# Eight experts in the order of their counts, three of them with stationary blocks of 64 high and 64 low columns, weights in rows of 4 KB, and a quarter of the weight residuals on GpSimd

## The chip, the cores and the metric

The kernel runs on one core of a Trainium2 chip. The metric is the device time of one execution in microseconds; the time before is the median of three runs. A difference of 0.2% (about 4 us) is what a measurement of this kernel can tell from none.

## What is computed

Two transformer blocks in a row on 256 tokens of width 1024, in fp32, each of two layers. The last layer of the second block ends in a mixture of experts, and only that part concerns the change:

```python
def swiglu(h, w_gate, w_up, w_down):
    a = jnp.einsum('bsd,df->bsf', h, w_gate)
    u = jnp.einsum('bsd,df->bsf', h, w_up)
    return jnp.einsum('bsf,fd->bsd', jax.nn.silu(a) * u, w_down)

logits = jnp.einsum('bsd,de->bse', h.astype(F32), w_router.astype(F32))
top_val, top_idx = lax.top_k(logits, TOP_K_EXPERTS)          # 2 of 8
top_w = jax.nn.softmax(top_val, axis=-1)
combine = jnp.sum(jax.nn.one_hot(top_idx, N_EXPERTS, dtype=F32) * top_w[..., None], axis=-2)
for e in range(N_EXPERTS):
    out = out + combine[..., e:e + 1].astype(h.dtype) * swiglu(h, w_gate[e], w_up[e], w_down[e])
```

Gate and up are 1024 x 2816 for each expert, down is 2816 x 1024: 34.6 MB an expert, 277 MB in all. An expert sees only the tokens that the router gives it, 64 of 256 on average.

## The kernel before

The program is written out by hand, one instruction stream per engine, with semaphores between them. What stands ahead of the experts (the four layers' projections and attention, three MLPs and the router, 1142 us) is the same before and after.

**Products in parts.** TensorE works on fp32r values. Each fp32 factor is split into a high part (a copy rounded to fp32r, made by ScalarE) and a low part (the factor less its high part, a subtraction on VectorE). A product of two factors is three matmuls: high x high, high x low, low x high (`product`). In the experts, the stationary operand is a block of 128 listed tokens and the moving one the weights, 512 columns at a time.

**Weights.** A weight tile is 128 x 2048 fp32 (1 MB). SyncE loads it in two halves of 512 KB into one of six raw slots (`raw(s)`, in `slab`; `MORE_RAW`), ScalarE writes `w_hi` (L1892), VectorE `w_lo` (L977) into one of three split slots, and TensorE uses both (L2351 to L2353). SyncE may refill a raw slot when `lo_dve` says that the subtraction is done, ScalarE may refill a split slot when `w_used` says that TensorE is through with it. An expert has 33 tiles. Gate and up are cut in steps of 512 inner columns (the first one 256), so a row of such a tile in HBM is 2 KB (the first 1 KB); rows of down are 4 KB.

**One expert.** For each step j of the inner width: up and gate products into banks 1 and 0 (`rows_up`), SiLU on ScalarE (L2279), the product of both on VectorE (L1757), a turn by TensorE (transposes, L2470), high and low parts of the turned hidden rows (`hid_hi` on ScalarE, L2179; `hid_lo` on VectorE, L1559), and the down products of step j - 1, which fill the time between (`sums`, into banks 2 and 3). The order on each engine is written out in `body`, for VectorE so:

```python
step(0, ahead=int(first))
if last:
    last_lists(n)
else:
    lists(2 * i + p + 1, n + 1)
step(1, ahead=1)
if not last:
    make_index(1 - p, n + 1, not first)
```

**Tokens.** `lists` compares each token's place with 0 to 127, which gives TensorE a matrix to find the listed tokens' numbers (`list_places`); `make_index` writes them; GpSimd fetches the 128 rows of the next expert by an indirect DMA (`fetch`, L918), and adds an expert's 128 output rows to `y_rows` in HBM by another (`scatter`, L924). This is all that GpSimd does in the experts. ScalarE scales the output with the token's weight (`output`, L2263). The experts come in the order 0 to 7, in a loop over pairs (`each_expert`). The last one's output is added on chip, and the sums of the other seven are read back and folded into x (`by_gate`, `fold`, L1713 and L1718). If an expert has over 128 tokens, everything runs a second time for the rest (`flag`).

In the layers ahead, GpSimd does make low parts, of whole tiles in four instructions of a quarter each (L826), and VectorE and GpSimd share the lot by tile.

## Time and profile before

| | before |
|---|---|
| median of 3 runs | 1914.62 us (1911.88 to 1915.4) |
| profiled execution, first to last instruction | 1912.1 us |
| experts in it | 1142.6 to about 1892.5 us, 750 us |
| one expert in its middle | 93.7 us |
| busy: TensorE, VectorE, ScalarE, GpSimd | 1824.1, 1416.6, 1122.6, 392.8 us |
| DMA | 506 MB, 265 GB/s on the mean, 380 in the experts |

The profiled execution's own time is given by its span alone, 2.5 us less than the median. The page says for each engine what it was busy, and follows the chain of waits that ended last; the groups give for each line of the kernel its busy time, the mean of one instruction and the idle time just ahead of it with what ended it. A wait costs something only on the engine that sets the end.

### The profile page before, as it was taken

How to read it: one execution, taken by the hardware profiler on the slowest of the kernel's cores; microseconds unless marked ns; L12 is line 12 of the kernel's file. 1: busy time of each engine (PE TensorE's matmuls, PEld its weight loads, DVE VectorE, ACT ScalarE, POOL GpSimd, SP SyncE). 2: the span in 40 equal slices, each digit the busy share in tenths (PEclk: the TensorE clock that was granted, in tenths of full speed). 3: DMA queues.
4: the chain of work that ended last, by engine and by line, in shares of the span. 5: the costliest groups of instructions: out<-in, count | busy, mean ns of one | idle time of the engine just before them, and what ended most of it. 6: DMA issues, size and time to landing. Idle time of an engine off the chain costs nothing.

```text
span 1912.1 us, 26024 instructions
## 1 busy us (share of the span) xinstructions
PE 1824.1 (95%) x8799; PEld 1486.2 (78%) x8799; DVE 1416.6 (74%) x1631; ACT 1122.6 (59%) x1296; POOL 392.8 (21%) x315
## 2 busy tenths in 40 slices
PE   7899999989999998899989879999999999999997
PEld 6678886868888786688878667888888888888885
DVE  5748874466976586644458758889888888888897
ACT  6745444564443464443345537777777777777775
POOL 3722203463212363200046500000000000000000
PEclk9999999999999999999999989999999999999999
DMA  8348884418987341455544258999999999999994
GB/s 271 111 161 327 343 342 147 149 54 323 344 347 275 91 152 45 154 195 179 192 154 142 69 187 334 386 376 386 380 384 376 383 383 381 380 374 381 381 387 167
DMA packets 237934, 506.45 MB, mean 265 GB/s; under 512 B 23304, under 2 KB 74720, under 8 KB 231712
## 3 DMA queue, kind: packets, MB, share of 16 engines
q1 hardware_dynamic: 225664, 492.91, 70.9%
q0 software_dynamic: 3008, 10.32, 2.0%
q10 hardware_dynamic: 9184, 2.23, 0.5%
q8 instruction: 43, 0.70, 0.1%
q14 instruction: 35, 0.29, 0.0%
HBM read 497.49 MB, written 7.91 MB: 264 GB/s over the span
## 4 chain that ended last, share of the span: by engine, by line
PE 83%; DVE 7%; issue 6%; ACT 3%; POOL 1%; DMA 0%; POOLq 0%; SPq 0%; DVEq 0%; ACTq 0%
PE bank L2351 25%; PE bank L2353 25%; PE bank L2352 25%; PE bank L2470 2%; ACT slab L2042 1%; PE bank L2789 1%; DVE slab L1290 1%; PE bank L2561 1%; PE bank L2539 1%; ACT w_hi L1892 1%; PE bank L2521 1%; POOL w_lo L826 1%; DVE x L1074 0%; PE bank L2572 0%; DVE slab L1271 0%
## 5 line engine op out<-in xcount | busy, mean ns | idle before, releaser
L977 DVE TENSOR_TENSOR w_lo<-slab,w_hi 128x2048 fp32r<-128x2048 f32 x369 | 847.8, 2308 | 214.3 <-ACT w_hi L1892 213.3
L1892 ACT ACTIVATE w_hi<-slab 128x2048 fp32r<-128x2048 f32 (+2 forms) x421 | 796.6, 1898 | 329.0 <-PE bank L2353 256.3
L2351 PE MATMUL bank<-w_hi,hT_hi 128*128 128x512 f32 (+3 forms) x1664 | 649.4, 390 | 14.2 <-DVE hT_lo L1012 4.4
L2352 PE MATMUL bank<-w_lo,hT_hi 128*128 128x512 f32 (+3 forms) x1664 | 638.0, 383 | 0.0
L2353 PE MATMUL bank<-w_hi,hT_lo 128*128 128x512 f32 (+3 forms) x1664 | 637.9, 383 | 0.0
L2351 PEld LDWEIGHTS bank<-w_hi,hT_hi 128*128 128x128 f32 x1664 | 316.0, 190 | 77.9 <-DVE w_lo L977 8.8
L2353 PEld LDWEIGHTS bank<-w_hi,hT_lo 128*128 128x128 f32 x1664 | 315.5, 190 | 59.7
L2352 PEld LDWEIGHTS bank<-w_lo,hT_hi 128*128 128x128 f32 x1664 | 316.3, 190 | 55.3
L826 POOL TENSOR_TENSOR w_lo<-slab,w_hi 128x512 fp32r<-128x512 f32 (+2 forms) x208 | 262.4, 1295 | 381.3 <-ACT w_hi L1892 361.6
L2351 PE MATMUL bank<-w_hi,hid_hi 128*128 128x512 f32 x680 | 265.6, 391 | 0.7 <-DVE w_lo L977 0.7
L2353 PE MATMUL bank<-w_hi,hid_lo 128*128 128x512 f32 x680 | 265.0, 390 | 0.0
L2352 PE MATMUL bank<-w_lo,hid_hi 128*128 128x512 f32 x680 | 264.5, 389 | 0.0
L2351 PEld LDWEIGHTS bank<-w_hi,hid_hi 128*128 128x128 f32 x680 | 127.6, 188 | 29.2 <-issue 2.3
L2353 PEld LDWEIGHTS bank<-w_hi,hid_lo 128*128 128x128 f32 x680 | 127.6, 188 | 26.7
L2352 PEld LDWEIGHTS bank<-w_lo,hid_hi 128*128 128x128 f32 x680 | 127.7, 188 | 26.3
L924 POOL DMA_INDIRECT y_rows<-slab,posi x7 | 16.6, 2367 | 515.6 <-ACT slab L2263 515.6
L901 POOL TENSOR_TENSOR slab<-slab 128x512 f32<-128x512 f32 x32 | 60.0, 1893 | 251.6 <-ACT slab L2188 251.6
L1577 DVE SCALAR_TENSOR_TENSOR big<-slab,csilu,big 128x2048 f32<-128x2048 f32 x42 | 103.5, 2473 | 0.0
L2042 ACT ACTIVATE slab<-slab,att 128x256 f32<-128x256 f32 x144 | 71.4, 499 | 52.3 <-DVE att L1271 43.0
L2179 ACT ACTIVATE hid_hi<-bank 128x512 fp32r<-128x512 f32 (+1 forms) x95 | 47.6, 527 | 46.1 <-PE bank L2470 46.1
L1290 DVE TENSOR_TENSOR slab<-slab,att 128x512 f32<-128x512 f32 x56 | 52.7, 942 | 5.8
L1271 DVE CUSTOM_DVE_ANT_0 slab<-bank,const 128x256 f32<-128x256 f32 x88 | 31.9, 417 | 33.4 <-PE bank L2521 33.3
(252 smaller groups left out, 1232.0 us busy)
## 6 DMA issues: line engine op xcount, KB each, us to landing
slab<-in_w_exp_gate SPq DMA_DIRECT2D x176, 512.0 KB, 7.0
slab<-in_w_exp_up SPq DMA_DIRECT2D x176, 512.0 KB, 7.5
slab<-in_w_exp_down SPq DMA_DIRECT2D x176, 512.0 KB, 7.1
slab<-in_w_ada SPq DMA_DIRECT2D x48, 1024.0 KB, 5.5
slab<-in_w_mlp_in SPq DMA_DIRECT2D x64, 512.0 KB, 5.4
slab<-in_w_mlp_out SPq DMA_DIRECT2D x64, 512.0 KB, 9.0
slab<-in_w_in SPq DMA_DIRECT2D x56, 512.0 KB, 5.0
slab<-in_w_out SPq DMA_DIRECT2D x32, 512.0 KB, 4.6
```

Source lines behind the costliest of these rows:

```text
L826: ins = pool.tensor_tensor(w_lo[:, q, o], raw(s)[:, o], w_hi[:, q, o].bitcast(F32), ALU.subtract)
L901: pool.tensor_tensor(scr(X_ACT2 + t * F_UP, F_UP), a, a, ALU.mult).then_inc(sq_done, 1)
L977: dve.tensor_tensor(w_lo[:, q, 0:n], raw(s)[:, 0:n], w_hi[:, q, 0:n].bitcast(F32), ALU.subtract).then_inc(lo_dve, 1)
L1290: dve.tensor_tensor(p, p, r[:, s, :].unsqueeze(2).broadcast_to([P, TT, SEQ]), ALU.mult).then_inc(nrm_done, 2)
L1577: ins = dve.scalar_tensor_tensor(acc, w, c, acc, ALU.mult, ALU.add)
L1892: act.activation(w_hi[:, q, 0:n], raw(s)[:, 0:n], ACT.Copy).then_inc(hi_done, 1)
L2042: act.activation(p, p, ACT.Exp, bias=att[:, 1, j, t:t + 1], scale=-1.0, accum_out=att[:, 2, j, t:t + 1]).then_inc(ex_done, 1)
L2179: act.activation(to_hi[:, f0:f0 + n, t * P:(t + 1) * P], src, ACT.Copy).then_inc(hidh_done, 1)
L2351: pe.matmul(dst, a_hi, b_hi, start=start, stop=False)
L2352: pe.matmul(dst, a_hi, b_lo, start=False, stop=False)
L2353: return pe.matmul(dst, a_lo, b_hi, start=False, stop=stop_)
L2470: ins = pe.transpose(dst[t][:, f * P:(f + 1) * P], scr(src + t * width_ + f * P, P), ident)
```

## The change

It reorders and recuts the experts. What stands ahead of them changes in nothing but the width of the first two expert tiles.

- **Order.** Expert 0 stays first. The other seven are sorted by their number of tokens: the four with most take places 1, 3, 5 and 7, the three with fewest 2, 4 and 6. The sort (`sort`, 25 small instructions) runs on VectorE in the first expert; SyncE reads the expert's number for each place from `order`.
- **Short experts.** Places 2, 4 and 6 hold at most 64 tokens. The 128 stationary columns are their 64 high and 64 low columns side by side, so that two matmuls (with `w_hi` and `w_lo`) give the whole product, with its high rows in partitions 0 to 63 and its low rows in 64 to 127. ScalarE moves the latter down, VectorE adds them, for gate and up. The down products of the third block of inner columns are done in the next body with three matmuls, with `hid_lo` set to zero. The output's two halves are added to `y_rows` by two indirect DMAs, the second after the first has landed.
- **Tiles.** The inner width is cut in three blocks of 768, 1024 and 1024 columns. A tile of gate or up holds two k rows of the whole block, so its rows in HBM are 3 or 4 KB. An expert has 36 tiles: eight of 1536 columns (the ones numbered -4 to 3 in a body), 26 of 2048, two of 1024 (18 and 19, a down chunk loaded in two halves of 64 partitions). The matmuls of the first block are 384 columns wide.
- **Low parts.** For the 27 tiles in `QUARTERED`, VectorE subtracts the first three quarters and GpSimd the last one; TensorE and SyncE wait for both.
- SiLU and the other steps on a block come in two halves, and the first expert of each round uses banks 6 and 7 for its second up block.

```diff
+E_WIDTH = (768, 1024, 1024)
+E_FROM = (0, 768, 1792)
+MS = len(E_WIDTH)
+MT = 36
+SHORT = P // 2
+SHORT_AT = (2, 4, 6)
+QUARTERED = tuple(range(0, 9)) + tuple(range(14, 18)) + (20,) + tuple(range(23, MT))
+ROUND_SUMS = 16 * (3 + 4 + 2 * 3)
...
+def down_chunks(j):
+    return ((0, 2), (2, 2), (4, 1), (5, 1)) if j == 0 else ((0, 2), (2, 2), (4, 2), (6, 2))
...
+def tile_width(r, first, last):
+    if r in (18, 19):
+        return D
+    return 2 * E_WIDTH[0] if r < 4 or first and r < 8 or r >= MT - 4 and not last else TILE
...
+                def wide_rows(w, j, n, r0):
+                    for b in range(4):
+                        to, loaded = slot_free(n, r0 + b)
+                        d = to[:, 0:2 * E_WIDTH[j]].rearrange("p (k n) -> p k n", k=2)
+                        for k in range(2):
+                            sp.dma_start(d[:, k:k + 1, :], w[:, 2 * b + k:2 * b + k + 1, E_FROM[j]:E_FROM[j] + E_WIDTH[j]]
+                                         ).then_inc(loaded, 16)
+                def down_rows(w, j, n):
+                    for b, (f, nf) in enumerate(down_chunks(j)):
+                        to, loaded = slot_free(n, down_tile(j) + b)
+                        d = to.rearrange("p (i n) -> p i n", i=2)
+                        at = E_FROM[j] // P + f
+                        for i in range(2):
+                            if nf == 2:
+                                sp.dma_start(d[:, i:i + 1, :], w[:, at + i:at + i + 1, :]).then_inc(loaded, 16)
+                            else:
+                                o = slice(i * P // 2, (i + 1) * P // 2)
+                                sp.dma_start(d[o, 0:1, :], w[o, at:at + 1, :]).then_inc(loaded, 16)
...
+                    if n == n0 + 1:
+                        sp.wait_ge(order_done, 1)
+                    wg, wu, wd = weights(0 if first else sp.value_load(order[0:1, n - n0:n - n0 + 1], min_val=0, max_val=NE - 1))
...
+    def scatter(n, n0):
+        turn_, at = n0 // NE, n - n0
+        pool.wait_ge(yo_done, 2 * (n - turn_) + 2)
+        done = sums_after(turn_, at // 2, at % 2)
+        for a, o in enumerate((slice(0, SHORT), slice(SHORT, P)) if at in SHORT_AT else (slice(0, P),)):
+            pool.wait_ge(scattered, done - (16 if at not in SHORT_AT else 32) + 16 * a)
+            pool.indirect_dma_start(y_rows, bass.IndirectOffsetOnAxis(index[n % 2][0:o.stop - o.start, 0:1], 0), y_out[o, :], None,
+                                    compute_op=ALU.add).then_inc(scattered, 16)
...
+    def last_quarter(n, r, first, last):
+        pool.wait_ge(hi_done, EXPERT0 + MT * n + r + 1)
+        w = tile_width(r, first, last)
+        o, s, q = slice(3 * w // 4, w), raw_slot(r), split_slot(r)
+        pool.tensor_tensor(w_lo[:, q, o], raw(s)[:, o], w_hi[:, q, o].bitcast(F32), ALU.subtract).then_inc(lo_pool, 1)
     def expert_rows(n0):
         for n in range(n0, n0 + NE):
-            p = n % 2
-            if n > n0:
-                scatter(1 - p, n - 1, n0)
-            if n < n0 + NE - 1:
-                fetch(1 - p, n + 1, n0)
-        sums_back(n0 // NE)
+            first, last = n == n0, n == n0 + NE - 1
+            def quarters(r0, r1):
+                for r in range(r0, r1):
+                    if quartered(r):
+                        last_quarter(n, r, first, last)
+            quarters(0 if first else -4, 10)
+            if not first:
+                scatter(n - 1, n0)
+            if last:
+                sums_back(n0 // NE)
+            quarters(10, 22)
+            if n == 0:
+                pool.wait_ge(rows_out, 32)
+            if not last:
+                fetch(n + 1, n0)
+            quarters(22, MT if last else MT - 4)
...
+            mark(dve.tensor_copy(rank_at[:, 0:1], iota[:, 0:1]))
+            mark(dve.tensor_copy(rank_at[:, 1:NE:2], iota[:, 1:1 + NE // 2]))
+            mark(dve.tensor_copy(rank_at[:, 2:NE:2], iota[:, 1 + NE // 2:NE]))
+            mark(dve.memset(spare, 0.0))
+            mark(dve.tensor_copy(counts[:, 1:NE], tot[:, 0, 1:NE]))
+            link(dve.memset(counts[:, 0:1], 2.0 * SEQ))
+            link(dve.memset(spare[:, 2:NE:2], float(P - SHORT)))
+            mark(dve.tensor_tensor(at, across(counts), down_(counts), ALU.is_gt))
+            link(dve.tensor_tensor(same, across(counts), down_(counts), ALU.is_equal))
+            link(dve.tensor_tensor(same, same, k_("earlier", NE, NE), ALU.mult))
+            link(dve.tensor_tensor(at, at, same, ALU.add))
+            link(dve.tensor_reduce(turns, at, AX.X, ALU.add))
+            link(dve.tensor_tensor(at, across(turns), down_(rank_at), ALU.is_equal))
+            each = at.unsqueeze(1).broadcast_to([P, TT, NE, NE])
+            for src, to in ((wts, ranked_wts), (pos, ranked_pos)):
+                link(dve.tensor_tensor(picked, each, src.unsqueeze(2).broadcast_to([P, TT, NE, NE]), ALU.mult))
+                link(dve.tensor_reduce(to, picked, AX.X, ALU.add))
+            link(dve.tensor_tensor(same, at, across(iota[:, 0:NE]), ALU.mult))
+            link(dve.tensor_reduce(turns, same, AX.X, ALU.add))
+            dve.tensor_copy(order[:, :], turns[0:1, :]).then_inc(order_done, 1)
...
+                def lows(r0, r1):
+                    for r in range(r0, r1):
+                        w, s, q = tile_width(r, first, last), raw_slot(r), split_slot(r)
+                        w = 3 * w // 4 if quartered(r) else w
+                        dve.wait_ge(hi_done, n * MT + (EXPERT0 + r + 1))
+                        dve.tensor_tensor(w_lo[:, q, 0:w], raw(s)[:, 0:w], w_hi[:, q, 0:w].bitcast(F32), ALU.subtract
+                                          ).then_inc(lo_dve, 1)
+                def activated(j):
+                    at = ub + n * (2 * MS) + 2 * j
+                    banks = (bank[6], bank[7]) if first and j == 1 else (bank[4], bank[5])
+                    w = half_of(j)
+                    if short:
+                        base = half_base(turn_, i, j)
+                        for c, o in enumerate(halves(j)):
+                            dve.wait_ge(half_moved, base + c + 1)
+                            dve.tensor_tensor(mact[0:SHORT, o], bank[c][0:SHORT, 0:w], mact[0:SHORT, o], ALU.add
+                                              ).then_inc(half_added, 1)
+                        for c, o in enumerate(halves(j)):
+                            dve.wait_ge(half_moved, base + c + 3)
+                            dve.tensor_tensor(up_low[:, o], banks[c][0:SHORT, 0:w], up_low[:, o], ALU.add
+                                              ).then_inc(half_added, 1)
+                        for c, o in enumerate(halves(j)):
+                            dve.wait_ge(act_done, at + c + 1)
+                            dve.wait_ge(half_added, base + c + 3)
+                            dve.tensor_tensor(mact2[0:SHORT, o], mact[0:SHORT, o], up_low[:, o], ALU.mult).then_inc(sq_done, 1)
...
+                lows(2 if first else -2, gate_tile(0, first) + 6)
+                activated(0)
+                if first:
+                    lows(10, 14)
+                else:
+                    lows(6, 10)
+                hidden_low(0)
+                if short:
+                    dve.wait_ge(w_used, FREE_SPLIT + EXPERT0 + n * MT + 8)
+                    dve.tensor_scalar(hid_lo[:, :, :], ones[:, 0:1].unsqueeze(2).broadcast_to([P, 4, SEQ]), 0.0, None, ALU.mult
+                                      ).then_inc(hid_zero, 1)
+                if first:
+                    dve.nop().then_inc(hid_zero, 1)
+                if first and n0 == 0:
+                    sort()
+                if not last:
+                    lists(ranked_pos, ranked_wts, SHORT if p == 1 else P, 2 * i + p + 1, n + 1)
+                lows(14 if first else 10, 18)
+                activated(1)
+                lows(18, 22)
+                hidden_low(1)
...
+                        if short:
+                            base = half_base(turn_, i, j)
+                            for c, o in enumerate(halves(j)):
+                                act.activation(mact[0:SHORT, o], bank[c][SHORT:P, 0:w], ACT.Copy).then_inc(half_moved, 1)
+                            for c, o in enumerate(halves(j)):
+                                act.activation(up_low[:, o], banks[c][SHORT:P, 0:w], ACT.Copy).then_inc(half_moved, 1)
+                            for c, o in enumerate(halves(j)):
+                                act.wait_ge(half_added, base + c + 1)
+                                act.activation(mact[0:SHORT, o], mact[0:SHORT, o], ACT.Silu).then_inc(act_done, 1)
+                        else:
+                            for c, o in enumerate(halves(j)):
+                                act.activation(mact[:, o], bank[c][:, 0:w], ACT.Silu).then_inc(act_done, 1)
...
+                def low_ready(r):
+                    pe.wait_ge(lo_dve, n * MT + (EXPERT_LO + r + 1))
+                    if quartered(r):
+                        pe.wait_ge(lo_pool, n * len(QUARTERED) + (EXPERT_POOL + quarters_before(r) + 1))
+                    return split_slot(r)
+                def both(dst, hi_, lo_, q, s, start, stop_):
+                    if lo_ is None:
+                        pe.matmul(dst, hi_, w_hi[:, q, s], start=start, stop=False)
+                        return pe.matmul(dst, hi_, w_lo[:, q, s], start=False, stop=stop_)
+                    return product(dst, hi_, lo_, w_hi[:, q, s], w_lo[:, q, s], start, stop_)
+                def rows_by(dst, j, r0):
+                    w = half_of(j)
+                    for b in range(4):
+                        q = low_ready(r0 + b)
+                        for k in (2 * b, 2 * b + 1):
+                            l_hi, l_lo = lhs_listed(k + KC * p, 0)
+                            for c in range(2):
+                                s = slice((k % 2 * 2 + c) * w, (k % 2 * 2 + c + 1) * w)
+                                ins = both(dst[c][:, 0:w], l_hi, None if short else l_lo, q, s, k == 0, k == KC - 1)
+                        ins.then_inc(w_used, 1)
...
+                inner(0)
+                gate(0)
+                if first:
+                    inner(1)
+                    pe.wait_ge(ix_made, 2 * n + 2)
+                    turn(0)
+                else:
+                    if p == 1:
+                        pe.wait_ge(hid_zero, i + (1 + (len(SHORT_AT) + 1) * turn_))
+                    sums(-1, False)
+                    turn(0)
+                    inner(1)
+                gate(1)
```

Two places in the instruction order show it. First VectorE, from the low parts of the first expert's hidden rows on. `w_lo<-slab,w_hi` is a subtraction for a weight tile, `listed_cols<-big` and `slab<-const,big` are the lists of the next expert. Before:

```order
L977 TENSOR_TENSOR w_lo<-slab,w_hi 128x2048 x2
L1559 TENSOR_TENSOR hid_lo<-bank,hid_hi 128x2x128
L977 TENSOR_TENSOR w_lo<-slab,w_hi 128x2048 x2
L1706 COPY listed_cols<-big 128x2
L1700 TENSOR_SCALAR slab<-const,big 128x128 x2
```

And now, from the 21st of the sort's 25 rows on; the first of them, L1805, stands right behind the low parts of the hidden rows (L1930):

```order
L1825 TENSOR_TENSOR big<-big 128x64
L1826 TENSOR_REDUCE big<-big 128x8
L1827 TENSOR_TENSOR big<-big 128x8
L1828 TENSOR_REDUCE big<-big 1x1
L1829 CAST posi<-big 1x1
L1837 COPY listed_cols<-big 128x2
L1839 TENSOR_SCALAR slab<-const,big 128x128 x2
L1888 TENSOR_TENSOR w_lo<-slab,w_hi 128x1536 x4
L1913 TENSOR_TENSOR big<-slab,bank 128x512 x2
```

The sort, L1805 to L1829, has come between the hidden rows and the lists, ahead of the subtraction for tile 14.

Then GpSimd, from the clearing of `y_rows` into the third expert. Before it had only DMAs there:

```order
L911 DMA y_rows<-big 128x3x1024
L918 DMA slab<-h_rows,posi 128x1024
L924 DMA y_rows<-slab,posi 384x1024
L918 DMA slab<-h_rows,posi 128x1024
L924 DMA y_rows<-slab,posi 384x1024
```

Now, from the addition of one long expert's output over a short expert to the two additions of that one's output:

```order
L997 DMA y_rows<-slab,posi 384x1024
L1010 TENSOR_TENSOR w_lo<-slab,w_hi 128x512 x5
L988 DMA slab<-h_rows,posi 128x1024
L1010 TENSOR_TENSOR w_lo<-slab,w_hi 128x512 x9
L1010 TENSOR_TENSOR w_lo<-slab,w_hi 128x384 x8
L1010 TENSOR_TENSOR w_lo<-slab,w_hi 128x512 x5
L997 DMA y_rows<-slab,posi 384x1024 x2
```

27 quarters of subtractions stand between one addition and the next, in the queue in which the DMAs wait.

## Rows read from the trace of the kernel before

**Rows 1.** The page: span, busy time and share of each engine; the chain by engine.

```profile
span 1912.1 us, 26024 instructions
...
PE 1824.1 (95%) x8799; PEld 1486.2 (78%) x8799; DVE 1416.6 (74%) x1631; ACT 1122.6 (59%) x1296; POOL 392.8 (21%) x315
...
PE 83%; DVE 7%; issue 6%; ACT 3%; POOL 1%; DMA 0%; POOLq 0%; SPq 0%; DVEq 0%; ACTq 0%
```

**Rows 2.** By window: busy us of PE, PEld, DVE, ACT, POOL; clock, DMA share, GB/s.

```profile
1353.24:1447.00 93.76, 93.76 (x432) 77.79 (x431) 83.84 (x54) 70.64 (x49) 3.34 (x2) 1.00 1.04 380
```

**Rows 3.** Waits, 1180 to 1880 us: us in total, times, longest.

```profile
ACT w_hi L1892 <- PE bank L2353: 100.1, 158, 1.2
DVE w_lo L977 <- ACT w_hi L1892: 71.2, 153, 0.9
...
PE bank L2351 <- DVE w_lo L977: 0.3, 1, 0.3
```

**Rows 4.** Groups of one expert: busy us, mean ns of one, idle before.

```profile
L977 DVE TENSOR_TENSOR w_lo<-slab,w_hi 128x2048 fp32r<-128x2048 f32 x34 | 77.5, 2292 | 9.9 <-ACT w_hi L1892 9.7
L1892 ACT ACTIVATE w_hi<-slab 128x2048 fp32r<-128x2048 f32 x33 | 63.3, 1917 | 13.3 <-PE bank L2353 13.3
```

**Rows 5.** TensorE in order of time: start us, us; two products, eleven starts apart.

```profile
1277.24 0.39 PE L2352 MATMUL bank<-w_lo,hT_hi 128*128 128x512 f32 x1
...
1279.76 0.39 PE L2351 MATMUL bank<-w_hi,hT_hi 128*128 128x512 f32 x1
```

**Rows 6.** View by window: indirect copies; only 2 KB rows; only 4 KB rows.

```profile
1352.00:1357.00 5.00, 5.00 (x28) 4.20 (x27) 4.92 (x4) 3.45 (x4) 0.00 (x0) 1.00 1.06 298
1377.00:1384.00 7.00, 7.00 (x33) 5.79 (x32) 6.13 (x4) 5.40 (x4) 0.00 (x0) 1.00 1.05 387
1414.50:1417.00 2.50, 2.50 (x12) 2.07 (x12) 2.08 (x2) 2.50 (x5) 0.00 (x0) 1.00 1.03 411
```

**Rows 7.** Groups, 1180 to 1880 us; the last row from 0 to 1150 us.

```profile
L1757 DVE TENSOR_TENSOR slab<-slab,bank 128x512 f32<-128x512 f32 x38 | 25.9, 681 | 0.9 <-issue 0.2
...
L2279 ACT ACTIVATE slab<-bank 128x512 f32<-128x512 f32 x37 | 22.2, 599 | 22.3 <-PE bank L2353 22.3
...
L1757 DVE TENSOR_TENSOR slab<-slab,bank 128x256 f32<-128x256 f32 x7 | 2.9, 413 | 0.0
...
L1892 ACT ACTIVATE w_hi<-slab 128x1536 fp32r<-128x1536 f32 x12 | 17.6, 1488 | 0.0
```

**Rows 8.** GpSimd beside VectorE at 163 us; then GpSimd's lines: min/median/max, four alone, mean.

```profile
163.25 5.62 POOL L901 TENSOR_TENSOR slab<-slab 128x512 f32<-128x512 f32 x2 [14.99 <-ACT slab L2188]
...
162.63 2.29 DVE L977 TENSOR_TENSOR w_lo<-slab,w_hi 128x2048 fp32r<-128x2048 f32 x1 [3.17 <-ACT w_hi L1892]
164.84 3.13 DVE L1577 SCALAR_TENSOR_TENSOR big<-slab,csilu,big 128x2048 f32<-128x2048 f32 x1
167.89 3.12 DVE L977 TENSOR_TENSOR w_lo<-slab,w_hi 128x2048 fp32r<-128x2048 f32 x1
170.94 2.34 DVE L1577 SCALAR_TENSOR_TENSOR big<-slab,csilu,big 128x2048 f32<-128x2048 f32 x1
...
L901 POOL TENSOR_TENSOR slab<-slab x32: 1034/1510/3200, 145.7 to 605.3; 128x512 f32<-128x512 f32 x32
...
120.66 5.01 POOL L826 TENSOR_TENSOR w_lo<-slab,w_hi 128x512 fp32r<-128x512 f32 x4
...
L826 POOL TENSOR_TENSOR w_lo<-slab,w_hi 128x384 fp32r<-128x384 f32 x48 | 50.6, 1088 | 67.0 <-ACT w_hi L1892 67.0
```

**Rows 9.** VectorE's small instructions behind the router, in order of time.

```profile
1129.00 0.29 DVE L1678 TENSOR_TENSOR slab<-slab,const 128x128 f32<-128x128 f32 x1
...
1129.97 0.17 DVE L1681 TENSOR_SCALAR big<-big 128x16 f32<-128x16 f32 x1
```

**Rows 10.** A fold instruction's group; landing of the additions to y_rows.

```profile
L1713 DVE TENSOR_TENSOR big<-big,rowg 128x1024 f32<-128x1024 f32 x2 | 2.4, 1218 | 0.0
...
DMA to landing us min/median/max: 9.9/10.5/10.9
```

More of the change, by code:

```diff
@@ new lines, in body @@
+                        short = is_short(p, first)
+                        def low_ready(r):
[8 more added lines that the diff above has]
+                            return product(dst, hi_, lo_, w_hi[:, q, s], w_lo[:, q, s], start, stop_)
@@ new lines, in turn @@
+                        def turn(j):
+                            nf = inner_chunks(j)
+                            banks = (bank[2], bank[3]) if first and j == 0 else (bank[0], bank[1])
+                            for f in range(nf):
+                                if f % (nf // 2) == 0:
+                                    pe.wait_ge(sq_done, ub + n * (2 * MS) + 2 * j + f // (nf // 2) + 1)
+                                src = mact2[:, f * P:(f + 1) * P]
+                                ins = pe.transpose(banks[f // 4][:, f % 4 * P:(f % 4 + 1) * P], src, ident)
+                            ins.then_inc(ht_done, 1)
```

520 lines of the change are left out of this document (290 added, 230 removed).

## Prediction

> **What bounds the kernel now.** I read the shares first [rows 1]: TensorE is busy 95% of the span and makes up 83% of the chain of waits that ended last. The diff touches the last third alone, from the router on: eight experts of 93.7 us each, 750 us together. One of them, in the view by window [rows 2], has TensorE busy 93.76 of 93.76 us, VectorE 83.8, ScalarE 70.6, GpSimd 3.3, and the DMA engines without a pause. The view of who waited for whom says which is the limit [rows 3]: ScalarE waits for TensorE to free a slot (100 us in 700), VectorE waits for ScalarE (71 us), TensorE waits for VectorE 0.3 us. So TensorE bounds it; VectorE has 10 us of slack in each expert, in which its 33 subtractions of 2.29 us are the bulk [rows 4].
>
> **What the change takes off TensorE.** One 512-column product starts every 0.229 us (eleven starts in 2.52 us [rows 5]). An expert has 396 of them. In a short expert (places 2, 4 and 6) the gate, up and first two down parts take two products in place of three: 116 fewer by full width, 26.5 us. The last down part keeps three, one of them with zeros. So TensorE would need 67 us in each of three experts and 93.7 in five; alone that would be 79 us. The rest must ask what is late next.
>
> **The loads.** An expert is 34.6 MB. Rows of 2 KB moved at 387 GB/s, rows of 4 KB at 411 [rows 6]; while the indirect copies run it was 298 for 5 us. At the new widths (3 and 4 KB) an expert takes 84 to 89 us, plus 4 for the two indirect copies: 89 us is the floor of an expert on the DMA side, 22 above TensorE's new 67. Loads alone would therefore leave the shorts little: some 7 us each, by the stock of six raw slots a little more.
>
> **VectorE and GpSimd.** This is where I expect the decision. 27 of an expert's 36 tiles are now quartered: VectorE subtracts three quarters, GpSimd one, both reading the raw tile and the high part from SBUF. VectorE's slope is (681 - 413) / 256 = 1.05 ns a column [rows 7], so 1536 columns cost 2.29 - 0.54 = 1.76 us, 1152 cost 1.35. If the quarters ran beside that, VectorE would fall from 75.6 to 62 us an expert. Do they? The trace has such a pair [rows 8]. At 163 us GpSimd runs two additions that take 1.03 us when alone, and VectorE runs instructions with two SBUF inputs. Both stretch: VectorE's scalar_tensor_tensor takes 3.13 us where the next, with GpSimd silent, takes 2.34; its weight subtraction takes 3.12, not 2.29; GpSimd's two take 5.62 together. Each GpSimd instruction costs VectorE its own length less 0.2 us. They take turns, they don't overlap. The Trainium skill's page "SBUF — State Buffer", section "Who interferes with whom", states that a VectorE instruction with two SBUF inputs and a GpSimd instruction that reads SBUF exclude each other for the whole instruction. The trace agrees in kind (5.62 us for what takes 2.1 alone) but shows 0.2 us less: by the page a wide quartered tile would take 1.76 + 1.25 = 3.01 us, a short expert some 6 us more, and the sum below would be 49 us in place of 32.
>
> A GpSimd quarter of 512 columns takes 1.25 us alone (four in 5.01), one of 384 on average 1.09 [rows 8]. So a quartered wide tile holds VectorE 1.76 + 1.03 = 2.79 us where the whole one held it 2.29, a narrow one 1.35 + 0.87 = 2.22 instead of 1.76. Per expert: 19 x 2.79 + 8 x 2.22 + 7 x 2.29 + 2 x 1.22 = 89.2 us, against 33 x 2.29 = 75.6 before. That is 14 us more, not 13 less.
>
> Other work of VectorE, by rows 7 (a 512-column instruction 0.68 us, 256 columns 0.41, 384 columns 0.55): in a long expert the products of the halves 3.8, low parts of the hidden rows 3.8, lists, index and listed rows 2.6: 10.2 us, as before. In a short expert each block has four additions and two products (6 x 0.55 + 12 x 0.68 = 11.5), low parts 2.4, clearing hid_lo 1.2, the rest 2.8: 17.9 us. Two allowances: consecutive instructions overlap a little (77.5 of subtractions and 10.2 of the rest were 83.8 us of busy time, so 3.9 off [rows 2, 4]); and a GpSimd quarter may run beside a VectorE instruction that reads a bank, at some six places an expert by up to 1 us, of which I take 5. Long: 89.2 + 10.2 - 8.9 = 90.5 us. Short: 89.2 + 17.9 - 8.9 = 98.2, and 0.8 for the chain from the last gate product through ScalarE's four copies to the next conversion: 99 us, bounds 92.5 (nearly all of it hidden) and 106 (none).
>
> ScalarE is no nearer: 63.3 us of high parts [rows 4], narrow ones 1.49 us [rows 7], and in a short some 15 us of copies and activations at 0.4 to 0.6: 79 us.
>
> **The sum.** A short expert then costs 99 - 93.7 = 5.3 us more than today, three of them 16. The long ones stay with TensorE but lose their slack: the round of a split slot is product 2.73 + high part 1.92 + low part 2.79 + some 0.3 of signals = 7.7 of the 8.2 us that three slots give, where it was 7.2; and ScalarE's silu and hidden copies now come in pairs of 0.60 [rows 7], 1.2 us at once, at some six places. I take 2 us for each of four, 8 us, between 0 and 16. The first expert has the sort: 25 small instructions on VectorE, 0.17 us to 0.29 each with 0.04 between [rows 9], 6.2 us, and the lists 0.7 behind it, ahead of tile 14's low part. TensorE has two tiles (5.5 us) in hand, of which the hidden rows' conversion uses 2.1: 2.1 + 6.9 + 1.8 - 5.5 = 5.3 us, once. In the last expert the four fold instructions of 1.22 us [rows 10] meet a VectorE without slack, and GpSimd must see two additions to y_rows land (10.5 us for 128 rows [rows 10], perhaps half for 64) before the quarter of tile 14: 3 us, between 0 and 9. The three clears of y_rows, the longer index names and SyncE's eight register loads come while six loaded slots cover them: nothing now; without that cover a few us. Sum: 16 + 8 + 5.3 + 3 = 32 us. The profiled span is 1912.1 us and the median of the runs 1914.6, so 2.5 us lie around it; both move alike: 1914.6 + 32 = **1947 us**.
>
> **Rivals.**
> 1. *Turns cost nothing here; the loads bound the short experts.* It would need the quarter to fall into VectorE's idle time, which after the change exists in shorts where DMA is late. For it: VectorE idles 10 us an expert today. Against: rows 8, and the 89.2 us of turns alone fill the 89 of the loads. Then a short takes the longest of ScalarE's 79, VectorE's 62 + 18 = 80 and the loads' 89 less 2 to 3 of stock: 86.5; three gain 21.6, the sort takes 5.3: 1898, between 1885 and 1910. The mechanism decides from the point where VectorE with its turns takes under 93.7 us in a short. Two tiles of each expert now load in halves of 64 partitions. The rows have no such load; I bound it by nothing and by the worst stretch, 1 MB at 298 in place of 411 GB/s, 1.0 us an expert, 3 us in all. The Trainium skill, "SBUF — State Buffer", section "Door 1: The DMA port swizzle", says 64 partitions reach 8 of 16 ports, 196 GB/s measured against 328, which would be an estimated 1.7 us an expert; no run here shows it.
> 2. *Everything but TensorE is hidden:* 79 us less, 5 back for the sort: 1841. It would need 34.6 MB in 67 us, 516 GB/s; the best stretch has 411.
> 3. *Half hidden.* GpSimd's quarters slip beside additions that read banks more often than I count and a short takes 92.5 to 94 us, long ones lose nothing: 1912 to 1925, at 1918.
> 4. *The waits feed TensorE's clock.* Granted clock is 1.00 throughout the experts [rows 2], that is 2.4 GHz. Waits of several us in the shorts could bring stretches at 1.2 GHz; three shorts with 5 us each more: above 1962.
> 5. *The round runs twice,* which would add some 750 us, if a short expert held over 64 tokens. The reference's router on its inputs gives 23, 54, 101, 78, 97, 44, 51 and 64 tokens; expert 0 stays first, the three smallest of the rest have 54, 51 and 44. I give it nothing.
>
> **How the numbers follow.** The forecast, 1926 to 1962, has 0.62; rival 3 0.12; rival 1 0.18; rival 2 0.02; rival 4 0.06. A difference under 0.2% (4 us) can't be told from none with this kernel. Below 1911: rivals 1 and 2, 0.20, and a corner of rival 3: 0.21. Within 1911 to 1918: half of rival 3, 0.07. Above: 0.72. For 8 in 10 the range takes the forecast's own, rival 3 and the upper half of rival 1: 1897 to 1962.
>
> **What would show it.** Right: VectorE's subtraction of 1536 columns at a mean near 2.5 to 2.8 us instead of 1.76, GpSimd's quarters near 2, VectorE and GpSimd together busy all through the shorts, TensorE waiting there for w_lo, periods of 99, 94 to 96 and, for the first expert, about 100 us. Wrong: subtractions at 1.76 us with GpSimd busy beside them, and shorts near 87 us in which ScalarE waits for DMA. The sort is right if TensorE has one wait of about 5 us in the first expert. Both DMA terms are wrong if 4 KB rows fall below 400 GB/s.

## The result, and the profile of the changed kernel

The changed kernel takes 1983.95 us (median of 4 runs, 1980.1 to 1988.2), the kernel before on the same chip 1913.25 (1909.9 to 1915.4): a ratio of 1.037, 95% interval 1.035 to 1.039. It is slower by 71 us, where 32 were forecast. The page, with the same parts as [rows 1]:

```profile
span 1978.3 us, 26060 instructions
...
PE 1790.4 (91%) x8619; PEld 1441.4 (73%) x8619; DVE 1446.2 (73%) x1715; ACT 1137.4 (57%) x1356; POOL 927.1 (47%) x536
...
PE 63%; DVE 14%; ACT 8%; POOL 7%; issue 6%; DMA 2%; DVEq 0%; SPq 0%; ACTq 0%; POOLq 0%
```

TensorE's share of the chain fell from 83% to 63%; VectorE, ScalarE and GpSimd took what it lost. Up to 1142 us the two traces run alike (TensorE busy 1068.6 us here, 1069.4 before), so all of it lies in the experts. The view by window, one expert each, cut where the last block's hidden rows are turned (line 3187): long, short, long, short. It answers to [rows 2].

```profile
1237.70:1336.90 99.20, 96.25 (x456) 80.19 (x455) 79.31 (x57) 70.62 (x52) 73.44 (x30) 1.00 0.98 360
1336.90:1439.50 102.60, 78.86 (x331) 59.55 (x330) 95.40 (x70) 75.65 (x64) 70.09 (x30) 0.95 0.96 349
1439.50:1539.20 99.70, 96.26 (x456) 80.25 (x455) 77.82 (x57) 70.31 (x52) 76.57 (x31) 1.00 0.97 358
1539.20:1640.80 101.60, 77.32 (x331) 57.27 (x330) 96.67 (x70) 75.79 (x64) 69.55 (x30) 0.98 0.96 351
```

A long expert takes 99 to 100 us where it took 93.8, a short one 102 to 103. Between the two profiled executions lie 66 us. The three longs and the three shorts in the middle lose 18 and 25 of them; some 24 are left for the first and last. The hidden rows of the last expert's last block are turned 102.2 us after those of the expert ahead of it; in the kernel before that was 91.8 us.

The subtractions of wide tiles as groups, 1142 to 1945 us, beside [rows 4]; the last row of the three is a whole tile on VectorE:

```profile
L1010 POOL TENSOR_TENSOR w_lo<-slab,w_hi 128x512 fp32r<-128x512 f32 x148 | 380.3, 2592 | 168.6 <-ACT w_hi L2483 168.3
L1888 DVE TENSOR_TENSOR w_lo<-slab,w_hi 128x1536 fp32r<-128x1536 f32 x147 | 329.9, 2262 | 64.0 <-ACT w_hi L2483 63.6
L1888 DVE TENSOR_TENSOR w_lo<-slab,w_hi 128x2048 fp32r<-128x2048 f32 x56 | 135.8, 2452 | 12.3 <-ACT w_hi L2483 12.1
```

Three quarters of a tile take VectorE nearly what the whole tile did (2.26 us against 2.29), and the quarter takes GpSimd 2.59 where it took 1.25 alone [rows 8]. In order of time, in a short expert where both always have a tile at hand (start, us, how many; consecutive ones are joined, their stretches overlap), the rhythm shows:

```profile
1408.58 18.45 POOL L1010 TENSOR_TENSOR w_lo<-slab,w_hi 128x512 fp32r<-128x512 f32 x7
```

```profile
1409.28 16.60 DVE L1888 TENSOR_TENSOR w_lo<-slab,w_hi 128x1536 fp32r<-128x1536 f32 x6
```

VectorE's six last 2.83 us each (1.76 alone) and start 2.76 apart: (16.60 - 2.83) / 5. That is the forecast turn of 2.79. Both engines show as busy, and yet they work nearly one after the other: alone the pair would take 1.76 + 1.25 = 3.01 us.

TensorE's waits from 1371.7 to 1472.5 us, of which the first 68 us belong to a short expert, whose two products stand in L3134 and L3135 (the rest is the long one behind it). In the kernel before, [rows 3] had 0.3 us of waits in 700:

```profile
PEld bank L3134 <- POOL w_lo L1010: 11.7, 8, 4.9
...
PEld bank L3134 <- DVE w_lo L1888: 9.1, 8, 3.0
PE bank L3134 <- POOL w_lo L1010: 8.6, 8, 4.4
PE bank L3134 <- DVE w_lo L1888: 8.1, 7, 2.5
```

### The profile page after: what moved, and what is told of

It is laid out like the page before. It is cut to its first block, busy times and chain, and to the rows that moved or that the text cites. A ratio compares the mean times of both kernels' runs of the same rounds, so it can differ in the third digit from the quotient of the medians.

```text
span 1978.3 us, 26060 instructions
## 1 busy us (share of the span) xinstructions
PE 1790.4 (91%) x8619; PEld 1441.4 (73%) x8619; DVE 1446.2 (73%) x1715; ACT 1137.4 (57%) x1356; POOL 927.1 (47%) x536
## 4 chain that ended last, share of the span: by engine, by line
PE 63%; DVE 14%; ACT 8%; POOL 7%; issue 6%; DMA 2%; DVEq 0%; SPq 0%; ACTq 0%; POOLq 0%
PE bank L2607 19%; PE bank L2609 18%; PE bank L2608 18%; POOL w_lo L1010 6%; DVE w_lo L1888 5%; ACT w_hi L2483 4%; ACT slab L2237 1%; PE bank L3045 1%; DVE slab L1381 1%; PE bank L2726 1%; DMA y_rows<-slab,posi 1%; PE bank L2817 1%; PE bank L2795 1%; PE bank L3134 1%; PE bank L3135 1%
## 5 line engine op out<-in xcount | busy, mean ns | idle before, releaser
L1888 DVE TENSOR_TENSOR w_lo<-slab,w_hi 128x1536 fp32r<-128x1536 f32 (+3 forms) x286 | 601.1, 2125 | 108.4 <-ACT w_hi L2483 107.4
L1010 POOL TENSOR_TENSOR w_lo<-slab,w_hi 128x512 fp32r<-128x512 f32 (+1 forms) x216 | 520.7, 2435 | 214.9 <-ACT w_hi L2483 214.6
L2607 PE MATMUL bank<-w_hi,hT_hi 128*128 128x512 f32 (+3 forms) x1448 | 556.6, 384 | 40.4 <-POOL w_lo L1010 12.3
L2609 PE MATMUL bank<-w_hi,hT_lo 128*128 128x512 f32 (+3 forms) x1448 | 545.8, 377 | 0.0
L2608 PE MATMUL bank<-w_lo,hT_hi 128*128 128x512 f32 (+3 forms) x1448 | 545.5, 377 | 0.0
L2607 PEld LDWEIGHTS bank<-w_hi,hT_hi 128*128 128x128 f32 x1448 | 275.5, 190 | 101.0 <-issue 21.3
L1068 DVE TENSOR_TENSOR w_lo<-slab,w_hi 128x2048 fp32r<-128x2048 f32 x105 | 245.5, 2349 | 136.3 <-ACT w_hi L2087 136.3
L2608 PEld LDWEIGHTS bank<-w_lo,hT_hi 128*128 128x128 f32 x1448 | 275.8, 190 | 40.7
L3134 PE MATMUL bank<-w_hi,hT_hi 128*128 128x512 f32 (+1 forms) x288 | 115.2, 400 | 35.3 <-POOL w_lo L1010 22.2
L3135 PE MATMUL bank<-w_lo,hT_hi 128*128 128x512 f32 (+1 forms) x288 | 108.6, 377 | 0.0
```

Source lines behind the costliest of these rows:

```text
L1010: pool.tensor_tensor(w_lo[:, q, o], raw(s)[:, o], w_hi[:, q, o].bitcast(F32), ALU.subtract).then_inc(lo_pool, 1)
L1068: dve.tensor_tensor(w_lo[:, q, 0:n], raw(s)[:, 0:n], w_hi[:, q, 0:n].bitcast(F32), ALU.subtract).then_inc(lo_dve, 1)
L1888: dve.tensor_tensor(w_lo[:, q, 0:w], raw(s)[:, 0:w], w_hi[:, q, 0:w].bitcast(F32), ALU.subtract).then_inc(lo_dve, 1)
L2607: pe.matmul(dst, a_hi, b_hi, start=start, stop=False)
L2608: pe.matmul(dst, a_hi, b_lo, start=False, stop=False)
L2609: return pe.matmul(dst, a_lo, b_hi, start=False, stop=stop_)
```

## The experiments

Theory A, mine: GpSimd's quarters take turns with VectorE and set the pace. Rivals came up as the runs asked for them: B and C, the loads; D, bursts of work at the ends of the wider blocks. Times are medians; each run was compared with the kernel before on its own chip, at 1911.8 to 1913.9 us.

| run | time, us | against before, interval |
|---|---|---|
| e1, no quarters | 1943.6 | 1.0132 to 1.0176 |
| e2, quarters in short experts only | 1976.2 | 1.0299 to 1.0347 |
| e3, quarters in long experts only | 1970.3 | 1.0281 to 1.0331 |
| e4, three products everywhere | 1977.7 | 1.0315 to 1.0358 |
| e5, that without quarters | 1949.0 | 1.0166 to 1.0218 |
| e6, loads over 128 partitions | 1983.8 | 1.0344 to 1.0397 |
| e7, that without quarters | 1937.3 | 1.0089 to 1.0150 |
| e8, e7 with three products everywhere | 1945.6 | 1.0151 to 1.0205 |
| e9, e7 with bursts later and apart | 1926.3 | 1.0059 to 1.0101 |
| e10, e8 with bursts later and apart | 1931.6 | 1.0080 to 1.0117 |
| e11, e9 with the sort spread | 1912.3 | 0.9995 to 1.0015 |
| e12, e9 with quarters back | 1989.5 | 1.0387 to 1.0431 |
| e13, e11 with the loop written out | 1915.3 | 0.9997 to 1.0034 |
| e14, e11 with rows of 2 KB | 1924.7 | 1.0049 to 1.0106 |
| e15, e6 with 16 columns for a quarter | 1943.9 | 1.0144 to 1.0191 |
| e16, e11 with two pieces moved off or ahead | 1913.0 | 0.9979 to 1.0007 |

**What the quarters cost (e1 to e3).**

```
-QUARTERED = tuple(range(0, 9)) + tuple(range(14, 18)) + (20,) + tuple(range(23, MT))
+QUARTERED = ()
```

> The changed kernel with QUARTERED empty: VectorE subtracts every tile whole, GpSimd none. Theory A (a quarter holds VectorE for its own length, and the low part of a tile is complete only when GpSimd, let in after the next instruction of VectorE, ends): subtractions return to 2.29 us, a long expert from 99.7 to 94 or 95 us, a short one from 102 to 90 (VectorE's 75.6 + 17.9 less overlap, and the loads' 87 to 89, both near it), the time to between 1905 and 1925. Theory B (the loads, whose rows, halves of 64 partitions and release of raw slots by SyncE are new, set the periods of 100 to 102): periods stay over 98, the time stays over 1965.

40 us came off, so B as put falls. But 30 us stayed, and the expected 1905 to 1925 was missed: without the quarters the periods are 96 to 99 us for both kinds, where I had the shorts at 90. So A is true and is not the whole. The two profiles are 33 us apart: the first expert gives back 5, the three middle longs 8, the three shorts 11, the last 9. In e2 and e3 `last_quarter` and VectorE split a tile at w - 16 in place of 3 * w // 4 in one kind of expert:

> As the changed kernel, but in the long experts GpSimd takes only 16 columns of each quartered tile and VectorE the rest; the short experts keep the quarter of 384 or 512. Theory A: long experts fall from 99.7 to 95 us or so, short ones stay at 102 (101 to 103): five long ones, three whole and the first and last in part, give back 20 to 28 us, 1956 to 1964. Theory B: nothing moves, 1978 to 1990.

> The reverse: quarters stay in the long experts, in the short ones GpSimd takes 16 columns. Theory A: short experts fall from 102 to 90 to 93 us, long ones stay at 99 to 100: 1948 to 1960. Theory B: nothing moves, 1978 to 1990. If the loss of the long ones is one of the shorts' queue passed on, the long ones shorten too and the time is under 1940.

Longs came to 97.7 to 99.1 (e2), shorts to 98.4 to 99.7 (e3). That is 8 and 14 us of 1984, in the direction of A, where A asked for 20 to 28 and for 24 to 36: both expectations were missed. The two don't add up to the 40 of e1, and why is open; that 16 columns keep part of the loss explains only some of it, as e15 shows, where all quarters are of 16 columns:

```profile
L1015 POOL TENSOR_TENSOR w_lo<-slab,w_hi 128x16 fp32r<-128x16 f32 x214 | 401.6, 1888 | 285.5 <-ACT w_hi L2488 285.2
L1893 DVE TENSOR_TENSOR w_lo<-slab,w_hi 128x2032 fp32r<-128x2032 f32 x152 | 342.0, 2278 | 45.4 <-ACT w_hi L2488 44.7
```

16 columns take GpSimd 1.89 us on the mean, since it waits out a VectorE instruction: the shortest takes 0.22 us, and nearly all end 0.08 us behind the end of a VectorE instruction. VectorE, at 2.28 us for 2032 columns, loses nothing. So a quarter has two prices: the time it holds VectorE, and the lateness of the low part that it completes. e15 weighs them:

> The changed kernel with loads over 128 partitions (1983.8 with quarters, 1937.3 without), with 16 columns on GpSimd in place of a quarter in every quartered tile. VectorE then loses no time worth the name, but a tile's low part is still complete only when GpSimd, which waits for the next instruction of VectorE to end, is done. If the quarters cost by VectorE's turns: within 10 us of the kernel without, 1937 to 1948. If by the lateness of the low part: over 1960.

1943.9 against 1937.3 without and 1983.8 with quarters: of the 46 us, the lateness that 16 columns bring is 7. The other 40 are the turns, with what a whole quarter ends later than 16 columns; no run parts these two.

**What the two products are worth (e4, e5, e8).** `is_short` returns False, with one addition to y_rows an expert:

> The changed kernel with quarters, 4 KB rows and sort, but every expert takes three products on 128 tokens (no short one, no additions of halves, one addition to y_rows an expert). Theory A: TensorE's 26.5 us a short expert were worth nothing, since VectorE and GpSimd set its pace; all experts take what the long ones take, 99.5 to 100: 1972 to 1982, a little faster than the changed kernel. A rival in which TensorE's saving counts and something else costs more: 2000 or above.

As expected: 1977.7, 6 us faster than with short experts. The 26.5 us that TensorE saves in each of three experts are worth less than nothing beside the quarters. Without the quarters they are worth 5 to 8 us in all (e5 against e1, e8 against e7).

> As the changed kernel without quarters, and with three products in every expert: what is left of the change is the tiles of 3 and 4 KB rows, the loads in halves of 64 partitions, the sort and the blocks of 768 and 1024 columns. Theory C (the four loads of 64 partitions per expert run at some 200 GB/s, with what is queued beside them, for 8 us, 4 us longer than at 411 GB/s, and the DMA engines have no pause to make it good): experts of 96 to 98 us, 1935 to 1950, as without quarters with short experts. If TensorE alone sets the pace: experts of 94.5 to 95, 1920 to 1926.

1949.0 is within C's range, but C is not what makes it, as the next runs say.

**The loads of 64 partitions (e6, e7).**

```
-o = slice(i * P // 2, (i + 1) * P // 2)
-sp.dma_start(d[o, 0:1, :], w[o, at:at + 1, :]).then_inc(loaded, 16)
+o = slice(i * COL, (i + 1) * COL)
+sp.dma_start(d[:, 0:1, o], w[:, at:at + 1, o]).then_inc(loaded, 16)
```

> The changed kernel, with quarters, but the two tiles of 128 weight rows per expert load as two halves of 512 columns over all 128 partitions in place of two halves of 64 partitions. Theory A (quarters set the periods): the stretch at 200 GB/s goes, 4 us of loading an expert with it, but the periods stay near 99 to 102: 1970 to 1984. Theory C (loads set them): 4 us an expert, 1945 to 1957.

> Without quarters and with the loads over 128 partitions. Theory C: the run without quarters at 1943.6 was bound by loads; 3 to 4 us an expert come off, 1912 to 1922. If VectorE and TensorE set its periods: under 8 us off, 1936 to 1944.

The same 8 us of a short expert by window, in e1 and then in e7 (the last number is GB/s):

```profile
1376.00:1384.00 8.00, 5.80 (x23) 3.79 (x21) 5.13 (x3) 4.67 (x5) 0.00 (x0) 1.00 1.02 205
```

```profile
1376.00:1384.00 8.00, 7.30 (x30) 4.84 (x29) 7.67 (x5) 6.94 (x5) 0.00 (x0) 1.00 1.04 407
```

The loads of 64 partitions do halve the rate, for 8 us an expert, 4 us lost. Yet with quarters it is worth 0 (1983.8 against 1984.0) and without 6 us of 1943.6. That the six raw slots cover the rest is my reading; no run changes their number. C falls; in e7 the periods are 96 to 97 us still.

> Neither quarters, short experts nor loads of 64 partitions: long rows, sort and wide blocks are left. Experts of 94 to 95 us and 5 us of sort: 1918 to 1928. Against the same with short experts (the run before this one) it says what a short expert is worth where neither quarters nor loads bind: 7 us each at most by the loads' 89 us, so up to 20 us; nothing if VectorE's 17.9 us of other work in a short expert takes it all.

This missed: 1945.6. The kernel that does the products of before has experts of 96.8 us, of which TensorE is busy 95.5, where it was 93.8 before:

```profile
1328.00:1424.80 96.80, 95.53 (x455) 80.75 (x454) 83.66 (x57) 70.96 (x52) 4.41 (x2) 1.00 0.97 370
```

Five waits stand in it, 1.3 us together and 0.4 the longest, where before had none. The suspects left are the wider blocks.

**Bursts at block ends (e9, e10).** One place in e7 shows it best, the end of a short expert: TensorE in order of time, then VectorE.

```profile
1417.76 0.39 PE L3135 MATMUL bank<-w_lo,hid_hi 128*128 128x512 f32 x1
1423.12 0.80 PE L3134 MATMUL bank<-w_hi,hid_hi 128*128 128x512 f32 x1 [4.97 <-DVE w_lo L1888]
1423.71 0.63 PE L3135 MATMUL bank<-w_lo,hid_hi 128*128 128x512 f32 x1
1424.14 0.63 PE L3134 MATMUL bank<-w_hi,hid_hi 128*128 128x512 f32 x1
```

```profile
1413.69 2.29 DVE L1888 TENSOR_TENSOR w_lo<-slab,w_hi 128x2048 fp32r<-128x2048 f32 x1 [0.27 <-ACT w_hi L2483]
1415.90 1.27 DVE L1900 TENSOR_TENSOR slab<-bank,slab 64x512 f32<-64x512 f32 x2
1417.10 1.27 DVE L1904 TENSOR_TENSOR big<-bank,big 64x512 f32<-64x512 f32 x2
1418.29 1.28 DVE L1909 TENSOR_TENSOR big<-slab,big 64x512 f32<-64x512 f32 x2
1419.49 1.27 DVE L1873 TENSOR_TENSOR hT_lo<-bank,hT_hi 128x512 fp32r<-128x512 f32 x2
1420.77 4.49 DVE L1888 TENSOR_TENSOR w_lo<-slab,w_hi 128x2048 fp32r<-128x2048 f32 x2
```

Eight instructions stand in VectorE's queue between two low parts, 4.9 us in which TensorE eats up its two tiles. After its wait of 5 us TensorE runs on at half speed: products start 0.43 us apart, not 0.227, and the windows of the wait, of the 5 us behind it and of the next 5.4 show the granted clock (the number before the DMA share):

```profile
1418.00:1423.00 5.00, 0.15 (x1) 0.00 (x0) 4.99 (x7) 5.00 (x5) 0.00 (x0) 0.86 0.91 355
1423.60:1428.60 5.00, 5.00 (x13) 3.89 (x13) 3.48 (x3) 1.79 (x2) 0.00 (x0) 0.52 0.87 288
1428.60:1434.00 5.40, 5.40 (x34) 5.18 (x34) 3.88 (x4) 3.50 (x4) 0.00 (x0) 1.00 0.91 312
```

0.52 is 1.2 GHz for nearly the whole stretch, then it is 2.4 again. The edit does the next tile first, then the work at a block's end in two pieces with a tile between them, and it is the same on ScalarE and VectorE (ScalarE's lines for block 1, shortened, without the first expert's numbers):

```
-highs(10, 18)
-activated(1)
-highs(18, 22)
+highs(12, 19)
+activated(1, 0)
+highs(19, 20)
+activated(1, 1)
+highs(20, 23)
```

> From the run without quarters and with loads over 128 partitions (1937.3): ScalarE and VectorE do the high and the low part of the next tile first and a block's activations, copies and hidden rows one tile later and in two pieces with a tile between them. Theory D (wide blocks of 768 and 1024 make bursts at the end of a block, for which TensorE, two tiles in hand, waits 0.4 to 0.7 us some five times in a long expert and 1.9 to 5.1 us in a short one): long ones go from 96.2 to 94 to 94.5, short ones from 96.2 to 92 to 94, 1917 to 1926. If VectorE's total of 89 us in a short one and small waits everywhere set it: over 1931.

> The same edit on the kernel with three products everywhere, without quarters, loads over 128 partitions (1945.6, experts of 96.8). Theory D: experts of 94 to 94.5, 1922 to 1930. If long rows or the order of the loads cost the 3 us of each expert: it stays over 1940.

11 and 14 us came off (1937.3 to 1926.3, 1945.6 to 1931.6), each a little short of what D asked. In e9 the shorts fell from 96 to 88 us, and the longs stood at 95 to 99.3: a long expert behind a short one now opens with a wait of 2.3 us for its listed rows. The 88 flatters the short: only 34 of its 36 subtractions still fall between the two marks. A short and the long behind it together take 186 to 187 us, where e7 had 192 and the kernel before 187.5. In e10 four of the six middle experts take 95.0 to 95.1 us in place of 96.8 (the other two 96.6 and 97.0, where e8 has 98.4 and 99.1):

```profile
1239.80:1334.80 95.00, 94.43 (x455) 80.91 (x454) 83.73 (x57) 71.25 (x52) 5.21 (x2) 1.00 1.00 377
```

The order is thus worth 1.8 of the 3 us that e8's experts lost. The other 1.2 stay: 0.6 us are waits, and TensorE is busy 94.4 us where it was 93.8. The narrow matmuls are an estimated 0.3 us of that: one of 384 columns starts 0.173 us after the one ahead (e10), where three quarters of the 0.227 of 512 columns would be 0.170, 96 times an expert.

**Quarters once more (e12).**

> The first of these with the quarters on GpSimd back. Theory A: the quarters hold VectorE in turns of 2.76 us a tile whatever the order of the rest, so short experts stay at 98 to 102 and the time is 1965 to 1980, 45 us or more above the same without quarters. Rival: the bursts made the quarters dear, and with the burst gone they cost under 20 us: 1925 to 1945.

1989.5: the range was missed upwards. With the bursts gone the quarters cost 63 us, not 40 to 46, so the rival falls, A stands, and the two causes hid one another. The kernel with quarters is even 6 us slower in the new order than in the old (e6). A short now takes 99.7 us, 11.5 more than in e9:

```profile
1339.60:1439.30 99.70, 77.52 (x331) 57.51 (x330) 92.09 (x66) 75.84 (x64) 75.00 (x30) 0.97 0.95 355
```

The longs behind a short go to 104.4 and 104.7 us. Why they lose that much, no run says; that lateness weighs more where the rest is tight is a guess.

**The sort (e11).** Its instructions are run four at a time behind the low parts of tiles 12 to 18. In the changed kernel it has this wait, and this clock in the window:

```profile
PEld bank L2607 <- DVE w_lo L1888: 6.9, 1, 6.9
PE bank L2607 <- DVE w_lo L1888: 6.5, 1, 6.5
```

```profile
1170.00:1180.00 10.00, 7.02 (x34) 5.51 (x33) 9.28 (x23) 6.69 (x6) 3.46 (x3) 1.00 1.04 288
1180.00:1190.00 10.00, 6.49 (x17) 5.15 (x18) 6.65 (x12) 0.91 (x1) 0.37 (x1) 0.66 0.79 270
```

> The first of these with the sort's instructions in fours behind the low parts of tiles 12 to 18 of the first expert, in place of all behind the hidden rows of its first block. TensorE's wait of 6.5 us and the stretch of 6.8 us at the lower clock behind it go: 6 to 9 us under the first of these. If the wait has another cause, no change.

14 us between the medians, and 10.3 between the profiled ends of the first expert. Of these, 4.4 are there before the sort begins: e9 had stretches at the lower clock just ahead of the experts and in their first products, and e11 not, which has nothing to do with the sort that I can show. The other 5.9 are 4.1 of wait and about 2 of half clock behind it. The rest of the 14 lies within the scatter of e9's four runs (1919.7 to 1928.7). The sort's own price is thus 6 us there; in the changed kernel, with its wait of 6.5 us and the stretch of half clock behind it, it is up to 10. e11 is level with the kernel before. Three of its experts by window, long, short, long:

```profile
1224.20:1319.20 95.00, 94.43 (x456) 80.90 (x455) 83.72 (x57) 70.81 (x52) 5.23 (x2) 1.00 1.00 376
1319.20:1407.60 88.40, 76.92 (x332) 57.80 (x331) 84.70 (x66) 74.07 (x64) 3.64 (x2) 0.98 1.02 392
1407.60:1506.80 99.20, 96.35 (x456) 82.51 (x455) 86.66 (x61) 71.28 (x53) 8.31 (x3) 0.98 0.99 370
```

The short one takes 88.4 us at 392 GB/s, with the DMA engines full (share 1.02) and VectorE busy 84.7 us of it: there the floor of 89 us for the loads is real.

**Rows of 4 KB, and what is left (e14, e13, e16).**

> The kernel with the sort spread, its tiles loaded in column halves, so in rows of 2 KB (1.5 KB for 768 columns) in place of 4 and 3 KB; as many DMAs of as many bytes. If long rows are what feeds its short experts of 88 us (387 GB/s in their windows): at some 370 to 387 GB/s the six in the loop average 95 in place of 92.7, 1922 to 1935. If rows of 2 KB do as well: 1909 to 1915.

1924.7: the long rows are worth 12 us where loads bind. With rows of 2 KB a short expert takes 92.1 us at 377 GB/s, in place of 88.4 at 392. In e13 the loop over pairs is written out, in e16 GpSimd clears hid_lo and the next expert's listed rows go ahead of the last products:

> The kernel with the sort spread (1912.3, no quarters, loads over 128 partitions, bursts apart), with the loop over three pairs of experts written out. TensorE waits there 2.4 us at each new pass of the loop, put down to issue, with its inputs ready. If that is the jump back to the loop's start: 5 to 7 us off, 1905 to 1908, under the kernel before. If it is the fetch of long code, it stays: 1910 to 1914, or grows.

> The kernel with the sort spread (1912.3), and in a short expert the clearing of hid_lo on GpSimd and the next expert's listed rows ahead of the last block's products. The 2.3 us that TensorE waits at the start of each long expert behind a short one end with the low parts of its listed rows, which stand late in VectorE's queue. If that order is the cause: 5 to 7 us off, 1905 to 1908, under the kernel before. If VectorE's total in a short expert is: under 3 us off, 1909 to 1913.

Neither moved the time (1915.3, 1913.0). In e13 the waits of 2.2 to 2.3 us stay, so they are no jump: by the view of waits they end with the low part of the listed rows. In e16 they shrink to 1.0 to 1.1 us and the longs behind a short to 96.5, while the shorts grow from 88 to 89 and the time stays. So the order of these two pieces is not what holds it; VectorE's total (171 us in a short and a long, in e11 as in e16) and the loads (share 1.02 in a short) are both left. No version beat the kernel before: e16 at 0.9993 (0.9979 to 1.0007) and e11 at 1.0005 can't be told from it.

## Why the prediction was wrong, step by step

The sign was right, the size was not: 71 us, outside of 1897 to 1962. From the changed kernel to e11 the whole difference is taken off in four edits: quarters 40.4, loads of 64 partitions 6.3, bursts 11.0, and 14.0 by the edit of the sort, of which the sort itself is 6 to 10; 71.7 in all; and e11 is 0.5 us over its kernel before. The shares hold in this order only, since the quarters weigh 40 in the first place and 63 in the last. By my terms, what is left without the quarters was to take 1905 to 1925 us (e1), and it took 1943.6: there lies most of the 37 us between 1947 and 1984. By experts, in the profiles: 25 us for the 16 forecast in the shorts, 18 for 6 in the three middle longs, 24 for 10 in the first and the last.

- **The turns: right.** 2.76 us measured for 2.79 (wide). GpSimd starting while VectorE runs still lets the two overlap a little, as [rows 8] said: alone they would be 1.76 + 1.25 = 3.01. An exclusive lock for the whole instruction, as the Trainium skill, "SBUF — State Buffer", section "Who interferes with whom", has it, would give these 3.01; the trace has 0.25 us less.
- **What the turns do to the experts: the total agrees in part by luck.** By my sum a short expert without quarters was 90 us, with them 99, and the longs lost 2: with the last expert's 3, some 38 us for the quarters, and e1 measured 40. But I had 27 of these in the three shorts, and the profiles have 11 there, since the shorts take 97 to 99 us without quarters, not 90 (e1). With the bursts moved, the shorts come out as the sums have them, 88 us without quarters (e9) and 99.7 with them (e12); the longs behind them, at 104 us in e12, do not.
- **The step that failed: "Short: 89.2 + 17.9 - 8.9", a sum of VectorE's work taken as a period.** It holds only if no one runs dry. TensorE has two tiles in hand, 3.7 us in a short expert, and VectorE's other work comes as 4 to 5 us at a time at the end of a block. Without quarters VectorE had 89 us of work in a short expert, as I had it, but the expert took 96 to 99 us. With the work moved one tile on and cut in two it took 88 (with 84.7 us of VectorE's work in it): the sum was right as a floor, and the queue's order kept it from being the period. With the quarters in, this hid in the total: a short took 102 to 103 for my 99, within my bounds.
- **Long experts: "I take 2 us for each".** Measured 5.9. Of these, 3.0 are there without quarters, shorts and loads of 64 partitions (96.8 us in e8): 1.8 go with the order of the bursts (95.0 in e10), and 1.2 are not taken apart. The other 2.8 come with the quarters (99.6 in e4). I had named the round of a split slot and the pairs of silus and hidden copies, and sized both together at a third.
- **Rival 4, the clock, had 0.06.** It happened in part: the granted clock was 0.95 to 0.98 in the shorts, that is half clock for some 3 to 10 us of each. It comes on top of the other waits, and should have been in the forecast.
- **The sort: 5.3 forecast,** 6.5 us of waiting and a stretch of half clock, 6 to 10 in all. The forecast's wait was 1.2 us short, and the clock was missing.
- **Loads of 64 partitions: 0 taken, 0 to 3 as bounds, and 1.7 us an expert by the Trainium skill's port rule.** The rate did halve (205 for 407 GB/s), in kind as the Trainium skill, "SBUF — State Buffer", section "Door 1: The DMA port swizzle", has it. It halved for longer than these loads alone would take: in the 8 us 1.6 MB moved, and they are 1.0 MB. That is 4 us of loading an expert. Under the quarters it cost nothing, without them 6 us.
- **The floor of 89 us for the loads, and 4 KB rows: right.** Shorts of 88 us in e11; 12 us were lost with rows of 2 KB (e14).
- **The last expert: 3 us forecast and 2 for it as a long one.** Between the turns of its last block and that of the expert ahead lie 102.2 us, for 91.8 before; without quarters (e1) it is 93.2. So the quarters cost 9 us there, at the upper bound that I had given. First and last together lost 24 us, the sort's 6 to 10 and these 9 among them; the rest isn't taken apart.

## What to carry to other kernels

Splitting an elementwise pass of two SBUF inputs between VectorE and GpSimd added work here (2.76 us a tile for 2.29): look in any trace for a place where the two meet, and price the pair as a sum. Adding up an engine's work gives a floor; the period is set by how much of its other work stands between two pieces that the next engine waits for, against the stock which that engine has. So put such work behind the urgent piece and cut it up. Price each long wait of TensorE with the half-speed stretch behind it.

## What the runs showed of the hardware that I had not expected

- A GpSimd subtraction of 16 columns takes 1.89 us beside VectorE's (e15), which at 2.28 us is not slowed: the price on VectorE goes with GpSimd's length, the delay on GpSimd does not.
- Four loads of 64 partitions, 1 MB together, pull down what is queued with them: 8 us at 205 GB/s, in which 407 moved twice as much.
- The long waits that a better order takes away are worth more than their length: behind one of 5 us the granted clock was 0.52 for 5 us (e7).
